# Rotary partners moved by small SBUF-to-SBUF transfers, and index stacks written by ScalarE and VectorE

## The reference

```python
h = rms_norm(x, g_mix[l])
proj = h @ w_in[l]
q, k, v, qi, ki, wi, conv_in, qc, gate_pre = split_cols(proj, PROJ_SIZES)
q = partial_rope(q.reshape(b, s, N_ATT_HEADS, HEAD_DIM), cos_a, sin_a)      # 6 heads of 64
k = partial_rope(k.reshape(b, s, N_KV_GROUPS, HEAD_DIM), cos_a, sin_a)      # 2 groups of 64
qi = partial_rope(qi.reshape(b, s, N_IDX_HEADS, IDX_DIM), cos_i, sin_i)     # 8 heads of 32
ki = partial_rope(ki, cos_i, sin_i)                                          # one head of 32
...
def partial_rope(x, cos, sin):            # half = head / 8 rows
    x1, x2, rest = x[..., :half], x[..., half:2 * half], x[..., 2 * half:]
    return concatenate([x1 * c - x2 * s, x2 * c + x1 * s, rest], axis=-1)
...
rel = relu(einsum('bqhd,bsd->bqhs', qi_b, ki))
score = einsum('bqh,bqhs->bqs', wi_b, rel) * idx_scale     # top 256 keys of each query by this score
```

## Time and profile before

| | us |
|---|---|
| median of 3 runs | 3115.48 (3112.72 to 3116.6) |
| the profiled execution | 3111.55 |
| its span | 3109.8 |
| PE busy | 2907.6 (93%) |
| DVE busy | 1689.6 (54%) |
| POOL busy | 1160.1 (37%) |
| ACT busy | 789.0 (25%) |

### The profile page before, as it was taken

One profiled execution on the slowest core, in us unless ns is written; L12 is line 12 of the kernel. 1 busy time (PEld: TensorE's weight loads), 2 busy tenths in 40 slices (PEclk: granted clock), 3 DMA queues, 4 the chain that ended last, 5 costly groups with the idle time before them and its releaser, 6 DMA issues.

```text
span 3109.8 us, 34850 instructions
## 1 busy us (share of the span) xinstructions
PE 2907.6 (93%) x13074; PEld 2347.0 (75%) x13074; DVE 1689.6 (54%) x2299; ACT 789.0 (25%) x1441; POOL 1160.1 (37%) x649
## 2 busy tenths in 40 slices
PE   7987999998899999999999889999798999999997
PEld 5675878886577788888888668878585888888885
DVE  3475899987554423233232638888846233333327
ACT  4055011114622201011020456666613000000003
POOL 2330334442033334333333416555432344433331
PEclk9978999998999999999999999999898999999998
DMA  3110122221051111111111110000020111111111
GB/s 146 41 34 7 48 68 77 79 81 61 1 190 41 41 48 48 47 48 53 47 47 48 62 74 28 21 28 26 16 95 28 48 48 47 47 47 53 48 47 61
DMA packets 45051, 165.37 MB, mean 53 GB/s; under 512 B 4880, under 2 KB 6160, under 8 KB 43920
## 3 DMA queue, kind: packets, MB, share of 16 engines
q1 hardware_dynamic: 37168, 129.31, 12.5%
q10 hardware_dynamic: 7776, 34.61, 2.9%
HBM read 147.12 MB, written 16.78 MB: 53 GB/s over the span
## 4 chain that ended last, share of the span: by engine, by line
PE 80%; DVE 12%; ACT 3%; issue 3%; DVEq 1%; DMA 0%; POOL 0%; ACTq 0%; SPq 0%; POOLq 0%
PE dense L558 21%; PE dense L559 21%; PE dense L562 21%; DVE stay L2060 2%; DVE a_lo L1638 2%; PE dense L978 2%; PE dense L979 2%; PE dense L980 2%; PE dense L598 1%; PE dense L599 1%; PE dense L600 1%; PE side L1016 1%; ACT T L1198 1%; PE side L1005 1%; DVE T L1617 1%
## 5 line engine op out<-in xcount | busy, mean ns | idle before, releaser
L467 POOL TENSOR_TENSOR w_hi<-raw,zero 128x1024 fp32r<-128x1024 f32 x210 | 400.8, 1909 | 1565.6 <-PE dense L562 1298.7
L558 PE MATMUL dense<-a_hi,w_hi 128*128 128x512 f32 x2000 | 783.6, 392 | 14.1 <-DVE T L1791 5.6
L559 PE MATMUL dense<-a_lo,w_hi 128*128 128x512 f32 x2000 | 780.3, 390 | 0.0
L562 PE MATMUL dense<-a_hi,w_lo 128*128 128x512 f32 x2000 | 617.5, 390 | 0.0
L469 POOL TENSOR_TENSOR w_lo<-raw,w_hi 128x1024 fp32r<-128x1024 f32 x210 | 526.1, 2505 | 16.5
L558 PEld LDWEIGHTS dense<-a_hi,w_hi 128*128 128x128 f32 x2000 | 377.0, 188 | 95.8 <-issue 7.7
L559 PEld LDWEIGHTS dense<-a_lo,w_hi 128*128 128x128 f32 x2000 | 376.8, 188 | 79.2 <-issue 1.2
L562 PEld LDWEIGHTS dense<-a_hi,w_lo 128*128 128x128 f32 x2000 | 376.6, 188 | 78.5
L558 PE MATMUL dense<-b_hi,w_hi 128*128 128x512 f32 x832 | 327.2, 393 | 5.2 <-DVE T L1966 2.5
L559 PE MATMUL dense<-b_lo,w_hi 128*128 128x512 f32 x832 | 324.7, 390 | 0.0
L1946 DVE TENSOR_TENSOR x_res<-x_res,dense 128x1024 f32<-128x1024 f32 x100 | 122.0, 1220 | 329.6 <-PE dense L562 328.3
(11 more groups left out here) (277 smaller groups left out, 4360.0 us busy)
## 6 DMA issues: line engine op xcount, KB each, us to landing
raw<-in_w_stream SPq DMA_DIRECT2D x231, 512.0 KB, 3.3
x_in<-in_x_t SPq DMA_DIRECT2D x8, 512.0 KB, 7.4
spill_gate<-T ACTq DMA_DIRECT2D x8, 512.0 KB, 2.6
spill_part<-gates ACTq DMA_DIRECT2D x8, 512.0 KB, 2.6
back<-spill_gate ACTq DMA_DIRECT2D x8, 512.0 KB, 3.7
back<-spill_part ACTq DMA_DIRECT2D x8, 512.0 KB, 4.6
x_res<-in_x_t ACTq DMA_DIRECT2D x2, 2048.0 KB, 9.0
spill_x<-x_res ACTq DMA_DIRECT2D x1, 4096.0 KB, 13.4
```

Of the source, the lines that this page charges most:

```text
L467: pool.tensor_tensor(w_hi[:, r % 2, :], raw[:, r, :], zero[:, 0:1].broadcast_to([P, D]), ALU.add).then_inc(weights_rounded, 1)
L558: pe.matmul(o, w_hi[:, slot, w], hi[:, k, x], start=b == 0, stop=False)
L559: pe.matmul(o, w_hi[:, slot, w], lo[:, k, x], start=False, stop=False)
L562: last = pe.matmul(o, w_lo[:, slot, w], hi[:, k, x], start=False, stop=stop)
```

## The change

- `swap_rows(t)` on ACT, behind the copy of tiles 0 to 6: a drain, then small DMA transfers within SBUF that put the partner rows into `T[:, 3 - t % 2]`: 2 of 4 rows for tile 0, 8 of 4 rows for each of tiles 1 and 2, 4 of 8 rows for each of tiles 3 to 6, each row 1024 floats. For tile 1 they stand behind the work on the memory's norm. The products of line 697 and their four matrices are gone, and with them the wait of PE for the tables.
- `rotate` on DVE multiplies that buffer in SBUF instead of `side`; for tile 0 on 32 rows only.
- `stack_high(t)` on ACT (after the copies of tiles 2, 3 and 4) writes the rounded pieces straight into the stacks: 2 copies of 32 x 1024 for the keys and 8 of 32 x 768 for each of the two query tiles. `stack_low(t)` on DVE writes the third piece: 1 and 4 subtractions. The selection products, their matrices and the 9 copies out of PSUM are gone.
- The meeting of the three engines is gone; in its place ACT waits for all rotations before step 0 and for the transposed values before step 1, and PE for DVE's copy of the values before step 1.
- PE takes 4 blocks of tile 8 (`BEFORE_INDEX`) before the transposes of the values; step n of the index loop then has block n+4, and steps 44 to 47 have none.

```diff
-MATRICES = ("ident", "ones", "swap_att", "swap_idx", "rep_ki", "rep_swap_ki", "causal_q", "strict_q")
+MATRICES = {"ident": 104, "ones": 104.5, "causal_q": 107, "strict_q": 107.5}
+BEFORE_INDEX = 4
+def swaps(t):
+    step, half, rows = (HD, HD // 8, P) if t >= T_K else (IDX_D, IDX_D // 8, IDX_D if t == T_KI else P)
+    return [(r + a * half, r + (1 - a) * half, half) for r in range(0, rows, step) for a in range(2)]
...
@@ tensor
                     pe.wait_ge(mem_scaled, KB)
-                    turn(0, T[:, 0, :], [(0, mats["rep_ki"]), (1, mats["rep_swap_ki"])])
-                    pe.wait_ge(turn_free[0], 1)
+                    emptied(pe, T_KI)
...
-                if t >= 2:
-                    turn(t - 1, T[:, (t - 1) % 2, :], [(t + 1, mats["swap_idx" if t - 1 < T_K else "swap_att"])])
-            emptied(pe, T_V)
...
-            meet(pe, "pe", met_n)
-            for n in range(IDX_H + 1):
...
-                    pe.matmul(side[0:STACK, n % 2, c:e], stack_mats[r, m, :], hi[r, c:e], start=True, stop=False)
-                    last = pe.matmul(side[0:STACK, n % 2, c:e], stack_mats[r, m + 1, :], lo[r, c:e], start=False, stop=True)
...
+            for b in range(BEFORE_INDEX):
+                memory_block(T_MEM, b)
+            emptied(pe, T_V)
...
+            pe.wait_ge(idx_split, 1 + IDX_H)
             for n in range(IDX_STEPS):
...
+                if n == 1:
+                    pe.wait_ge(att_v_taken, 1)
...
-                memory_block(T_MEM + n // KB, n % KB)
+                m = n + BEFORE_INDEX
+                if m < IDX_STEPS:
+                    memory_block(T_MEM + m // KB, m % KB)
@@ scalar
+            def swap_rows(t):
+                act.drain()
+                for to, at_row, rows in swaps(t):
+                    act.dma_start(T[to:to + rows, 3 - t % 2, :], T[at_row:at_row + rows, t % 2, :]).then_inc(swapped[t % 2], 16)
+            def stack_high(t):
+                if t == T_KI:
+                    for block in (0, 1):
+                        last = act.activation(ki_stack[IDX_D * block:IDX_D * block + IDX_D, :], ki_f[0:IDX_D, :], ACT.Copy)
...
+                for h in range(4):
+                    for block in (0, 2):
+                        last = act.activation(qi_stack[IDX_D * block:IDX_D * block + IDX_D, 4 * (t - T_QI) + h, :],
+                                              qi_f[IDX_D * h:IDX_D * h + IDX_D, t - T_QI, TOPK:S], ACT.Copy)
...
                 act.activation(T[:, t % 2, :], dense[:, t % 2, :], ACT.Copy).then_inc(sums_free[t % 2], 1)
+                if t < T_V and t != 1:
+                    swap_rows(t)
...
+                if 2 <= t < T_K + 2:
+                    stack_high(t - 2)
-            meet(act, "act", met_n)
...
-                act.activation(ki_stack[0:STACK, :] if n == 0 else qi_stack[0:STACK, n - 1, :],
-                               side[0:STACK, n % 2, 0:S if n == 0 else IDX_S], ACT.Copy).then_inc(stack_copied, 1)
...
@@ vector
-                dve.wait_ge(turned, n_turned)
-                dve.tensor_tensor(T[:, 2 + t % 2, :], side[:, v % 2, :], rope_tab[:, tab + 1, :], ALU.mult
-                                  ).then_inc(turn_free[v % 2], 1)
-                dve.tensor_tensor(T[:, t % 2, :], T[:, t % 2, :], rope_tab[:, tab, :], ALU.mult)
+                dve.wait_ge(swapped[c], 16 * sum(len(swaps(u)) for u in range(c, t + 1, 2)))
+                dve.tensor_tensor(T[r, other, :], T[r, other, :], rope_tab[r, tab + 1, :], ALU.mult)
+                dve.tensor_tensor(dst, T[r, c, :], rope_tab[r, tab, :], ALU.mult)
                 dve.drain()
-                dve.tensor_tensor(dst, T[:, t % 2, :], T[:, 2 + t % 2, :], ALU.add).then_inc(roped, 1)
+                return dve.tensor_tensor(dst, dst, T[r, other, :], ALU.add)
```

More of the change, by code:

```diff
@@ L223, in build @@
         T = at("T", [P, 4, S], F32, 88)
-        mats = {name: at(name, [P, P], F32, 104 + 0.5 * n) for n, name in enumerate(MATRICES)}
+        mats = {name: at(name, [P, P], F32, kib) for name, kib in MATRICES.items()}
         ident, ones = mats["ident"], mats["ones"]
@@ L436, in _ @@
             sp.dma_start(small[:, :], io["small"]).then_inc(consts_in, 16)
-            for name in MATRICES[:2]:
+            for name in tuple(MATRICES)[:2]:
                 sp.dma_start(mats[name][:, :], io[name]).then_inc(consts_in, 16)
@@ L686, in _ @@
             spread(0, 0)
-            def turn(n, src, matrices):
-                for m, (v, matrix) in enumerate(matrices):
-                    if m == 0:
-                        emptied(pe, n)
-                    if v >= 2:
-                        pe.wait_ge(turn_free[v % 2], v // 2)
-                    for c in range(0, S, 512):
-                        last = pe.matmul(side[:, v % 2, c:c + 512], matrix[:, :], src[:, c:c + 512], start=True, stop=True)
-                    last.then_inc(turned, 1)
             for t in range(T_KI, T_MEM):
@@ L761, in _ @@
             pe.wait_ge(parts["mem"][1], KB)
+            for b in range(BEFORE_INDEX):
+                memory_block(T_MEM, b)
+            emptied(pe, T_V)
+            for b in range(TB):
+                last = pe.transpose(side[:, 1, b * P:b * P + P], T[:, T_V % 2, b * P:b * P + P], ident[:, :])
+            last.then_inc(att_v_turned, 1)
+            pe.wait_ge(idx_split, 1 + IDX_H)
             for n in range(IDX_STEPS):
@@ L1169, in memory_copy @@
                 act.activation(dst, dense[:, u % 2, 0:width], ACT.Copy).then_inc(sums_free[u % 2], 1)
-            act.activation(ki_hi[:, :], ki_f[:, :], ACT.Copy).then_inc(idx_round, 1)
-            for t in range(2):
-                act.activation(qi_hi[:, t, :], qi_f[:, t, TOPK:S], ACT.Copy).then_inc(idx_round, 1)
-            for n in range(IDX_H + 1):
-                act.wait_ge(stacked, n + 1)
-                act.activation(ki_stack[0:STACK, :] if n == 0 else qi_stack[0:STACK, n - 1, :],
-                               side[0:STACK, n % 2, 0:S if n == 0 else IDX_S], ACT.Copy).then_inc(stack_copied, 1)
             for n in range(IDX_STEPS):
@@ new lines, in stack_low @@
+            def stack_low(t):
+                if t == T_KI:
+                    dve.wait_ge(idx_round, 1)
+                    dve.tensor_tensor(ki_stack[2 * IDX_D:STACK, :], ki_f[0:IDX_D, :], ki_stack[0:IDX_D, :].bitcast(F32),
+                                      ALU.subtract).then_inc(idx_split, 1)
+                    return
+                for h in range(4):
+                    n = 4 * (t - T_QI) + h
+                    dve.wait_ge(idx_round, n + 2)
+                    dve.tensor_tensor(qi_stack[IDX_D:2 * IDX_D, n, :], qi_f[IDX_D * h:IDX_D * h + IDX_D, t - T_QI, TOPK:S],
+                                      qi_stack[0:IDX_D, n, :].bitcast(F32), ALU.subtract).then_inc(idx_split, 1)
@@ L1700, in _ @@
+            rotate(T_KI, ki_f[0:IDX_D, :], IDX_D)
+            dve.wait_ge(wi_turned, 1)
+            dve.tensor_copy(tiny[:, 160:160 + TB * IDX_H], side[:, 0, 0:TB * IDX_H])
             dve.drain().then_inc(roped, 1)
@@ L2283, in constants @@
     c = {"ident": np.eye(P), "ones": np.ones((P, P))}
-    def partner(d, half):
-        return np.where(d % (8 * half) < half, d + half, d - half)
-    def swap(half):
-        m = np.zeros((P, P))
-        turn = r[r % (8 * half) < 2 * half]
-        m[partner(turn, half), turn] = 1
-        return m
-    c["swap_att"], c["swap_idx"] = swap(8), swap(4)
-    c["rep_ki"] = (r[:, None] == r[None, :] % IDX_D).astype(float)
-    c["rep_swap_ki"] = c["swap_idx"][:, r % IDX_D] * (r[:, None] < IDX_D)
     c["causal_q"] = np.where(r[None, :] <= r[:, None], 0.0, NEG)
     c["strict_q"] = np.where(r[None, :] < r[:, None], 0.0, NEG)
-    same, to = r[:, None] % IDX_D == np.arange(STACK)[None, :] % IDX_D, np.arange(STACK)[None, :] // IDX_D
-    c["stack_mats"] = np.concatenate([same * np.isin(to, g) for g in ((0, 1), (2,), (0, 2), (1,))], axis=1)
     tab = np.zeros((P, 4, S), np.float32)
```

71 lines of the change are left out of this document (23 added, 48 removed).

## The result

| us | before | after |
|---|---|---|
| median | 3116.04 (3112.72 to 3116.99) | 3081.09 (3077.36 to 3081.54) |
| profiled execution, its span | 3111.55, 3109.8 | 3077.36, 3075.6 |
| PE starts tile 0's side products | 77.42 | 77.35 |
| first index product | 170.36 | 135.89 |
| end of the mask additions | 245.62 | 213.26 |

The ratio is 0.9886, with a 95% interval of 0.9866 to 0.9905. One of the four executions was disturbed and took 7352.89 us (none of the 40 later executions of kernels with such transfers was like it); it is left out of the ratio and of the range, but the median counts it, and without it the median is 3080.63. The same kernel on another chip gave 3080.42 against 3115.04, again 0.9886 (0.987 to 0.9903).

The account below looks back on a forecast made before the run. PE's permutation work bounds up to tile 7, nothing for long behind it, then DVE and later PE in the loop. 33.6 us gained ahead less 0.4 in the loop is 33.2: median 3082 us, range 3078 to 3086.

Parts of the forecast that it names:

- Up to the loop: From PE's start at 77.42 to the first index product: loop starts at 136.8 in place of 170.36, gaining 33.6 us.
- The split of the gain, 14.1 and 19.4: Of the 33.6 us, 14.1 are permutation products on PE and 19.4 the stage behind tile 7.
- Issue: Issuing one small transfer on ACT: 0.4 us each, giving ACT 9.1 of 10.9 us at tiles 3 and 4.
- the sign to look for: In the profile after, the partners should have landed within 5 us of ACT's issue.
- The rival with ACT as the bound: ACT's queue bounds the tiles: at 1.48 us an issue, some 10.6 us lost in all, 3093 us; chance 0.12.
- Landing: Small transfers within SBUF take 2 to 3 us to land; still hidden if eight land singly, 1.9 each.
- rarer, not more frequent: Rotations at later tiles: partners land about 5 us behind the tile's end, past POOL's 4.3 us, so fewer DVE-POOL collisions.
- Tile 0, the thinnest place: Rotation waits for POOL until 81.96; ACT's copy of tile 2 done at 87.2, wanted by PE at 90.1: 2.9 to spare.
- The loop: Index loop to the end of the mask additions, 75.3 us before: +0.4 together, neither gaining nor losing.
- Its tail: From PE's last block to the end of the mask additions: 12.3 us in place of 6.65, +5.65.
- the one for the clock (-1.2): First loop steps ran below full clock after the idle stage: five steps 0.25 us longer each, now gone, -1.2.
- "Nothing is changed behind the loop": Everything behind the index loop only shifts; a change over 2 us from mask additions to run's end would show it wrong.

Follow-up runs that it names:

- e1_rotate: Kernel before with only the transfers and the new rotation; selection products, their copies and the meeting kept: 3097.08 us against 3113.61, ratio 0.9951.
- e5_transfers2: Changed kernel with each small transfer cut along its columns into two, 68 in place of 34, same bytes: 3089.70 us, ratio 0.9925 to the kernel before.
- e8_psumrelu: Changed kernel with the relu written in place into PSUM, PE waiting for DVE's use: 3073.38 us, ratio 0.9867 to the kernel before; its repeat 3071.22, 0.9861.
- e7_actround: Changed kernel with ACT in place of POOL rounding the weights of tiles 10 to 15: 3073.29 us, ratio 0.9869 to the kernel before.

## Why the prediction was right, and where it was off

3082 was forecast and 3081.09 measured; for the profiled execution 3078.4 and 3077.36. The mechanism was the one forecast: the permutations left the path and their work was hidden, and the stage behind tile 7 went. By its steps:

- **Up to the loop: 33.6 forecast, 34.5 measured.** Tiles 3 to 7 follow each other without a wait, tile 7 ends at 133.66 (133.8 forecast), the loop starts at 135.89 (136.8). The 0.9 is the transposes: I carried over the 1.5 us from ACT's copy to their end, and they stood there behind that copy; now the blocks hide it and the loop starts 0.79 after the first transpose.
- **The split of the gain, 14.1 and 19.4, was wrong by about 3** although the sum was right. The 22.4 us behind tile 7 contained the rotation of tile 6, whose removal is the transfers' work: e1_rotate alone brings 16.7. I had put it all down to the stacks.
- **Issue: 0.4 us each forecast, 0.61 to 0.66 measured**, half as much again and more, between my two rows (0.34 and 1.48). Therefore tile 2's partners were there 6.5 us after the first issue (8 x 0.4 and 2 to 3 for the landing make 5.2 to 6.2; the sign to look for said within 5), and ACT's load at tiles 3 and 4 was 10.7 of 10.9 us, not 9.1. It cost nothing, since ACT's copies were over 6 us ahead of PE. The rival with ACT as the bound, given 0.12, needs dearer issues: with everything else as in the trace I estimate that tile 7 begins to wait at about 1.0 us for an issue ((122.9 - 116.24) / 16 more than 0.61, the sixteen issues between the copies of tiles 2 and 5). e5_transfers2, with twice the number, is over that point.
- **Landing: 2 to 3 us forecast, 1.2 to 3.3 measured** behind the last issue of a group, by DVE's waits in the traces (101.57 less 100.04 is one, and 111.22 less 108.27, tile 4's, another). The Trainium skill, "DMA: Bandwidth & Descriptors", section "Rules for kernel authors", calls transfers under 64 KB mostly overhead; the traces agree, since an issue takes 0.61 us for 16 KB and for 4 KB alike.
- **Collisions: "rarer, not more frequent" was wrong.** At tiles 2 to 5 at least one operation of each rotation is stretched, at tiles 4 and 5 two of three. My step had the partners land 5 us behind a tile's end, between two splits. But ACT made the stacks' copies first and copied tile 4 out only at 104.56, over 3 us behind its end at 101.1; DVE had its partners at 111.22, 10.1 us behind the end, and POOL's next split began at 112.15. Tile 2 was later still, since its copy had to wait for the rotation of tile 0. The time was there (50.66 of 58.54 us busy on DVE), so the sum stood.
- **Tile 0, the thinnest place**, was as forecast: DVE stood until 83.0 and ACT's copy of tile 2 ended at 86.72 (87.2 forecast, 90.1 allowed).
- **The loop: +0.4 forecast, +2.1 and +1.6 measured.** Its tail was right: 12.2 us from PE's last block to the end of the mask additions (12.3 forecast). Its first part shortened by 3.4 and not by 5.3. The term that was off is the one for the clock (-1.2). The first steps did run at full clock, 0.98 to 1.00 up to 145.00, but from 140.00 on PE was busy for 2.12 us of 5.00 only, behind DVE, which stood beside POOL's split, and then the clock fell, as these rows of the kernel after show:

```profile
140.00:145.00 5.00, 2.12 (x12) 1.59 (x11) 4.81 (x3) 1.19 (x3) 4.18 (x2) 0.98 0.21 81
145.00:150.00 5.00, 4.68 (x17) 4.30 (x18) 3.62 (x6) 3.42 (x7) 0.00 (x0) 0.50 0.31 105
```

  Behind its first score operation DVE waits 8.8 us for ACT's relus in this loop, where it waited 5.8 before. e8_psumrelu bears this out, as its loop keeps the full clock once the standstill is gone; how much of the missing 1.9 us is the clock alone no run shows.

- **"Nothing is changed behind the loop"** holds as far as the traces can tell: the part behind it was 1.8 us shorter in one trace of the changed kernel and 1.4 longer in the other.

The nearly exact sum thus owes something to luck: +0.9 up to the loop against -1.7 in it, and the +1.8 of one execution in the profiled time. The Trainium skill's rule in "SBUF — State Buffer", section "Who interferes with whom", which in the prediction changed nothing in the sum up to the loop, turned out to be the largest thing left. It holds for VectorE instructions with two inputs in SBUF; e8_psumrelu agrees with it, as moving one of DVE's two operands out of SBUF ended the standstill of the score operations, 17.2 us of DVE's time in the loop.

## What to carry over

Count a small transfer at what its issue costs the engine that issues it, and add that to this engine's load per tile; the landing matters once, for the group. When a stage is taken off the path, look which engine's order had late work queued ahead of the stage's first step, since that belongs to another part of the change. And where DVE and POOL both work from SBUF in the loop that bounds, moving one of DVE's operands to PSUM can be worth more than taking work away; here it was 9 us of the loop for a few changed lines.

## What was not expected of the hardware

- **A copy on ACT costs by its columns, not by its partitions.** Eight copies of 32 x 768 took 6.88 us, 0.86 each, those of 96 x 768 0.807, and one of 32 x 1024 took 1.07 (2.13 / 2) where one of 128 x 1024 took 1.03. The narrow ones read SBUF and the wide ones PSUM, so the small differences say nothing of the partitions. Three pieces written apart are three times the price of one copy, on two engines; it was hidden here.
- **Behind the same idle stretch the clock comes back at different moments.** Ahead of the first convolution tile PE is idle for 4.5 us in both kernels. Before, the granted clock then stays at 0.50 for two stretches of 2.5 us; after, it is 0.63 in the first and 0.69 in the second. The first of them, before:

```profile
299.30:301.80 2.50, 2.48 (x6) 2.02 (x7) 0.23 (x1) 2.45 (x3) 0.00 (x0) 0.50 0.00 0
```

and after, at the same products:

```profile
267.03:269.53 2.50, 2.48 (x7) 2.04 (x8) 0.23 (x1) 2.45 (x3) 0.00 (x0) 0.63 0.00 0
```

From the first product of this tile to the first of the sparse attention's logits it is 426.5 us before and 425.0 after. The traces fall into two groups: 426.5 to 426.6 before and in e1_rotate, e7_actround, e8_psumrelu and its repeat, and 424.2 to 425.0 in the others, both traces of the changed kernel among them. This follows no part of the change, since e7_actround and e8_psumrelu contain all of it. Why the rise falls where it does was not settled.
